# Head of a one-core decoder layer: a third weight tile in a bank of its own and split in pieces, a weight tile moved up in the stream, and products of ones between the first products

## The reference, cut to what matters

```python
def reference(x, c, ..., ada_w, ada_b, norm1_g, w_in, ...):
    sc = jax.nn.silu(c)
    mod = sc @ ada_w[l] + ada_b[l]
    sh1, sc1, g1, sh2, sc2, g2 = [m[:, None, :] for m in jnp.split(mod, 6, axis=-1)]
    xn = rmsnorm(x, norm1_g[l]) * (1.0 + sc1) + sh1          # x is (1, 256, 1024)
    proj = xn @ w_in[l]
    q, k, v, ca, cg = jnp.split(proj, ...)                   # attention: q, k, v; convolution: ca, cg
    ...                                                      # attention over 8 heads
    a = ca * jax.nn.sigmoid(cg)
    a = causal_dwconv(a, conv_dw_w[l], conv_dw_b[l])         # 31 taps
    a = jax.nn.silu(group_norm(a, ...))
    x = x + g1 * (jnp.concatenate([y_attn, a], axis=-1) @ w_out[l])
    xn2 = rmsnorm(x, norm2_g[l]) * (1.0 + sc2) + sh2
    h = causal_dwconv(xn2 @ w_up[l], ...)
    u, g = jnp.split(h, 2, axis=-1)
    return x + g2 * ((jax.nn.silu(g) * u) @ w_down[l])
```

## Time and profile before

| | |
|---|---|
| median of 3 runs | 360.16 us (360.15, 360.16, 363.2) |
| the profiled execution | 365.96 us |
| its span, first to last instruction | 364.2 us |
| mean granted TensorE clock in it | 0.975 of full speed |
| PE busy | 350.2 us, 96% of the span |
| DVE, ACT, POOL busy | 262.5, 177.3, 49.2 us |
| DMA | 79.51 MB, mean 218 GB/s |
| first matmul of conv 2, the end of the head | 46.46 us |

### The profile page before, as it was taken

How to read it: one execution, slowest core, us unless ns; L and a number is a source line. 1 busy time by engine, 2 the same in 40 slices (tenths; PEclk the granted TensorE clock), 3 DMA queues, 4 the chain that set the end, 5 groups by cost and what they waited for, 6 DMA issues and landing times.

```text
span 364.2 us, 6185 instructions
## 1 busy us (share of the span) xinstructions
PE 350.2 (96%) x2425; PEld 299.4 (82%) x2425; DVE 262.5 (72%) x489; ACT 177.3 (49%) x259; POOL 49.2 (14%) x77
## 2 busy tenths in 40 slices
PE   7789999999999998998999999999999999999995
PEld 6557878887664486886998989898989999998984
DVE  2652689979999758648887785766676675858566
ACT  5442662335206484657567645536455463645520
POOL 6362062205001602003200000000000000000000
PEclk9977999999999889999999999999999999999999
DMA  7999947979998991160355556455454554500003
GB/s 281 425 424 422 414 147 297 367 282 342 376 402 289 370 413 53 65 230 2 130 218 200 162 222 226 142 206 193 163 221 142 209 195 165 219 2 1 2 0 115
DMA packets 12797, 79.51 MB, mean 218 GB/s; under 512 B 1368, under 2 KB 2784, under 8 KB 3552
## 3 DMA queue, kind: packets, MB, share of 16 engines
q1 hardware_dynamic: 12560, 78.97, 57.4%
q10 hardware_dynamic: 144, 0.13, 0.1%
q0 software_dynamic: 64, 0.01, 0.0%
HBM read 78.05 MB, written 1.06 MB: 217 GB/s over the span
## 4 chain that ended last, share of the span: by engine, by line
PE 89%; DMA 3%; DVE 3%; issue 2%; ACT 1%; SPq 1%; POOL 0%; DVEq 0%; ACTq 0%; POOLq 0%
PE bank L945 25%; PE bank L946 24%; PE bank L947 24%; PE bank L969 5%; DMA raw<-in_stream 3%; PE bank L1000 2%; PE bank L1202 2%; PE bank L1212 1%; PE bank L1092 1%; DVE w_lo L603 1%; PE bank L1014 1%; PE bank L1238 1%; PE bank L1135 1%; PE bank L1224 1%; PE bank L1145 0%
## 5 line engine op out<-in xcount | busy, mean ns | idle before, releaser
L945 PE MATMUL bank<-act_hi,w_hi 128*128 128x256 f32 x480 | 138.6, 289 | 4.1 <-issue 1.3
L946 PE MATMUL bank<-act_lo,w_hi 128*128 128x256 f32 x480 | 136.6, 285 | 0.0
L947 PE MATMUL bank<-act_hi,w_lo 128*128 128x256 f32 x480 | 136.5, 284 | 0.0
L603 DVE TENSOR_TENSOR w_lo<-raw,w_hi 128x2048 fp32r<-128x2048 f32 (+1 forms) x44 | 95.1, 2161 | 27.6 <-ACT w_hi L374 27.6
L945 PEld LDWEIGHTS bank<-act_hi,w_hi 128*128 128x128 f32 x480 | 92.8, 193 | 12.8 <-issue 9.1
L946 PEld LDWEIGHTS bank<-act_lo,w_hi 128*128 128x128 f32 x480 | 93.0, 194 | 0.4
L947 PEld LDWEIGHTS bank<-act_hi,w_lo 128*128 128x128 f32 x480 | 92.9, 194 | 0.0
L374 ACT ACTIVATE w_hi<-raw 128x2048 fp32r<-128x2048 f32 x45 | 85.8, 1908 | 11.0 <-DMA raw<-in_stream 8.7
L690 DVE SCALAR_TENSOR_TENSOR bank<-glu,cols,bank 128x256 f32<-128x256 f32 x116 | 46.4, 476 | 0.0
L562 ACT ACTIVATE bias<-bank,cols 128x256 f32<-128x256 f32 x44 | 22.2, 556 | 33.9 <-PE bank L947 33.9
L945 PE MATMUL bank<-w_hi,hid_hi 128*128 128x512 f32 x88 | 34.8, 396 | 0.0
(11 more groups left out here) (177 smaller groups left out, 399.2 us busy)
## 6 DMA issues: line engine op xcount, KB each, us to landing
raw<-in_stream SPq DMA_DIRECT2D x71, 1024.0 KB, 6.0
xt<-in_x_t SPq DMA_DIRECT2D x2, 512.0 KB, 4.6
bias<-toeplitz_rows SPq DMA_DIRECT2D x1, 1024.0 KB, 10.7
xr<-in_x_rows SPq DMA_DIRECT2D x1, 1024.0 KB, 8.2
out<-xmod SPq DMA_DIRECT2D x3, 256.0 KB, 2.0
gates_b<-in_ada_b_gates SPq DMA_DIRECT2D x1, 256.0 KB, 8.6
cols<-in_cols SPq DMA_DIRECT2D x1, 185.0 KB, 5.4
out<-xmod SPq DMA_DIRECT2D x1, 128.0 KB, 1.9
```

What stands on the lines that cost most here:

```text
L603: nc.vector.tensor_tensor(w_lo[:, m % PARTS, cut], slot(*SPLIT[m])[:, cut], w_hi[:, m % PARTS, cut].bitcast(f32), ALU.subtract).then_inc(l ...
L945: nc.tensor.matmul(o, sh, mh, start=first, stop=False)
L946: nc.tensor.matmul(o, sh, ml, start=False, stop=False)
L947: return nc.tensor.matmul(o, sl, mh, start=False, stop=last)
```

## The change

- The stream has conv 1 ahead of modulation slot 2, as the fourth slot.
- The squares: ACT squares tiles 4 and 5 as well as 0 to 3, DVE only 6 and 7.
- All `act_lo` of the head go to DVE. POOL has instead the last 768 columns of conv 1 and conv 2 (`POOL_LOW` from 1), and fills the bias rows in one go.
- DVE multiplies `xt` by the inverse norm one part ahead; the low part of conv 0 beyond its first quarter is made after the low parts of `xn` 0 and 1.
- ACT and DVE take conv 1 in pieces at k = 1, and conv 2 in a piece of 768 columns at k = 6 and one of 1280 at k = 7 (ACT), around k = 7 (DVE).
- A sigmoid of a spare element stands on ACT after the last `act_hi`.
- PE has other places for the products of conv 0 and conv 1, with `ada_columns(k)` between them from k = 4 on; part k - 1 follows modulation slot k. `keep_clock` is products of ones, in five places (2, 8, 2, 6 and 2 of them), and the warming ahead of the squares is 10 products.
- conv 2 writes bank 6 and waits for no `glu_ready`.

```diff
-STREAM = [("ada", 0), ("conv", 0), ("ada", 1), ("ada", 2), ("conv", 1),
+STREAM = [("ada", 0), ("conv", 0), ("ada", 1), ("conv", 1), ("ada", 2),
...
-POOL_LOW = range(3, 13)
+POOL_LOW = range(1, 13)
...
+CONV_OF = (0, 1, 6, 1)
+FIRST_PIECE = 3 * SLOT // 8
...
-            for k in range(POOL_LOWS):
-                if 1 <= k <= 3:
-                    fill_rows(buckets[9 * (k - 1):9 * k])
-                pool.wait_ge(xn_full, k + 1)
-                pool.wait_ge(xn_hi, k + 1)
-                nc.gpsimd.tensor_tensor(act_lo[:, k, :], xmod[:, k, :], act_hi[:, k, :].bitcast(f32),
-                                        ALU.subtract).then_inc(xn_lo_pool, 1)
...
+            low_rest(1)
+            fill_rows(buckets)
...
             nc.scalar.activation(xmod[:, 0:KT // 2, :], xt[:, 0:KT // 2, :], ACT.Square).then_inc(xsq_left, 1)
+            act.wait_ge(xt_right, 16)
+            nc.scalar.activation(xmod[:, KT // 2:KT - 2, :], xt[:, KT // 2:KT - 2, :], ACT.Square).then_inc(xsq_right, 1)
...
             copy_rows(0)
-            split_hi_first(0)
-            for k in range(KT):
-                if k == 3:
-                    split_hi_first(1)
-                if k >= 1:
-                    copy_rows(k)
-                if k == KT - 1:
-                    split_hi(FIRST)
+            hi_first_piece(0, PIECE)
+            xn_high(0)
+            hi_other_piece(0, PIECE)
+            copy_rows(1)
+            hi_first_piece(1, PIECE)
+            xn_high(1)
+            hi_other_piece(1, PIECE)
+            for k in range(2, KT):
+                copy_rows(k)
+                if k == KT - 2:
+                    hi_first_piece(FIRST, FIRST_PIECE)
+                elif k == KT - 1:
+                    hi_other_piece(FIRST, FIRST_PIECE)
                 xn_high(k)
+            nc.scalar.activation(spare[:, 0:1], eps[:, :], ACT.Sigmoid)
...
+            xhat(0)
+            xn(0)
+            lo_first_piece(0, PIECE)
+            xn_low(0)
+            xhat(1)
+            xhat(2)
+            xn(1)
+            lo_first_piece(1, PIECE)
+            xn_low(1)
+            lo_other_piece(0, PIECE)
+            xhat(3)
+            lo_other_piece(1, PIECE)
+            xn(2)
+            xn_low(2)
+            for k in range(3, KT):
+                if k + 1 < KT:
+                    xhat(k + 1)
+                xn(k)
+                xn_low(k)
+                if k == KT - 2:
+                    lo_first_piece(FIRST, FIRST_PIECE)
+            lo_other_piece(FIRST, FIRST_PIECE)
...
-                    nc.tensor.transpose(bank[to][:, 0:P], ident[:, :], ident[:, :])
+                    nc.tensor.matmul(bank[to][:, 0:P], ones[:, :], ones[:, :], start=True, stop=True)
...
             ada_rows(0)
+            keep_clock(2, 5)
             ada_columns(0)
-            keep_clock(16, 5)
+            keep_clock(8, 5)
             ada_rows(1)
             first_products(0, (0,))
+            keep_clock(2, 5)
             ada_columns(1)
+            keep_clock(6, 5)
+            first_products(0, (1,))
+            first_products(1, (0,))
             ada_rows(2)
+            first_products(1, (1,))
             ada_columns(2)
-            first_products(1, (0,))
-            first_products(2, (0,))
             ada_rows(3)
-            first_products(0, (1,))
+            keep_clock(2, 2)
             ada_columns(3)
-            first_products(1, (1,))
-            ada_rows(4)
-            first_products(2, (1,))
-            ada_columns(4)
-            for k in range(5, KT):
+            first_products(2)
+            for k in range(4, KT):
                 ada_rows(k)
-                first_products(k - 2)
+                first_products(k - 1, (0,))
                 ada_columns(k)
-            first_products(KT - 2)
+                first_products(k - 1, (1,))
             first_products(KT - 1)
...
-                pe.wait_ge(glu_ready, j - 1)
-                pair(m, j % 2)
+                if j > FIRST:
+                    pe.wait_ge(glu_ready, j - 1)
+                pair(m, CONV_OF[j])
```

More of the change, by code:

```diff
@@ L341, in gn_square @@
                                         conv[:, 2 * g:2 * g + 2, :], ALU.mult).then_inc(gn_sq, 1)
-            for m in POOL_LOW:
+            low_rest(1)
+            fill_rows(buckets)
+            pool.wait_ge(rows_filled, 2 + len(buckets))
+            pool.dma_start(toeplitz_rows, bias_rows[:, :]).then_inc(rows_stored, 16)
+            for m in POOL_LOW[1:]:
                 if m == SP_AT["out", 0]:
@@ L425, in conv_gate @@
                     act.wait_ge(glu_ready, j - 1)
-                nc.scalar.activation(glu_gate[:, j % 2, :], bank[j % 2][:, 0:SEQ], ACT.Sigmoid).then_inc(sig_ready, 1)
+                nc.scalar.activation(glu_gate[:, j % 2, :], bank[CONV_OF[j]][:, 0:SEQ], ACT.Sigmoid).then_inc(sig_ready, 1)
             def qk_raw_out(j):
@@ L656, in norm2_columns, with xhat, xn @@
                 dve.wait_ge(mod_cols_read, 2)
-            for k in range(KT):
+            def xhat(k):
                 nc.vector.tensor_tensor(xt[:, k, :], xt[:, k, :], rinv[:, :], ALU.mult).then_inc(xhat_ready, 1)
+            def xn(k):
                 norm1_columns(k)
@@ L698, in after @@
                     dve.wait_ge(sig_ready, j + 1)
-                    nc.vector.tensor_tensor(glu[:, j, CONV_TAPS - 1:], bank[4 + j if j < FIRST else j % 2][:, SEQ:2 * SEQ],
+                    nc.vector.tensor_tensor(glu[:, j, CONV_TAPS - 1:], bank[4 + j if j < FIRST else CONV_OF[j]][:, SEQ:2 * SEQ],
                                             glu_gate[:, j % 2, :], ALU.mult).then_inc(glu_ready, 1)
@@ L1029, in first_products @@
                     elif k == 2:
-                        ready(m)
+                        pe.wait_ge(lo_done, m + 1)
+                        pe.wait_ge(hi_done, m + 1)
+                    elif k == POOL_FROM // (2 * P) and m in POOL_LOW:
+                        pe.wait_ge(lo_rest, POOL_LOW.index(m) + 1)
                     for c in range(2):
```

47 lines of the change are left out of this document (18 added, 29 removed).

## The result

| | before | changed |
|---|---|---|
| median of 4 runs each | 361.68 us (360.15 to 366.45) | 368.4 us (364.39 to 369.01) |
| the profiled execution | 365.96 us | 368.93 us |
| its span, mean clock | 364.2 us, 0.975 | 366.1 us, 0.977 |
| conv 2's first matmul | 46.46 us | 45.23 us |

A forecast was written before the change was run, and what follows sets the result against it. PE was taken as the bound, with idle gaps and half clock in the head left to win: conv 2 at 42.2 instead of 46.46 us takes 4.3 us off the 360.16 median, giving 356.0 us, range 353.9 to 361.2.

The forecast's parts named there:

- The first product: After slot 1's rows: PE starts at 15.8 us instead of 17.03, a gain of 1.2 us at this point.
- the ones: 20 products in five places of the head: 0.24 us each, 0 us together, or 2 to 3 us at 0.47.
- the clock up to 36 us: Head of PE: granted clock 1.00 from 5 to 36 us, the sum's main step.
- The middle: Conv 1 through part 2: POOL's conv 1 columns beside DVE cost 0.8 us; slot 4 starts between 26.4 and 27.2.
- the second reading of the two: POOL and DVE beside each other on conv 1: each blocks the other, so the middle slips 1.4 us, to 27.8.
- The landing of conv 2: Conv 2 lands at 35.9 us, ACT wants it about 33.7; PE idles up to 1.7 us after slot 7's rows.
- POOL's share of conv 2: POOL's 768 columns start at 38.9 and end between 40.8 and 42.0 us, in time with little to spare.
- The clock behind the gap: Rival, chance 0.13: gaps moved to 36.2 and 39.8 us bring a 3.4 us dip at 0.50, costing 1.7 us: 357.7.
- the slower rival: Chance 0.09: clock falls behind ACT's wait for conv 2, which starts at 47.1 to 48.2; 360.8 to 361.9 us, or 365.5.
- Carrying the 4.3 us over to the median: Head gain taken off the 360.16 us median, 5.8 us below the profiled execution: 355.9, say 356.0 us.
- The first rival: Chance 0.24: median runs of before lack the head's dip, so the change gives -0.4 to +1.1 us, 359 to 360.6.
- The sum over the profiled execution: Conv 2 starts at 42.2 instead of 46.46, 4.3 us off the head: 365.96 - 4.3 = 361.7 us.

The follow-up runs named there:

- e8: The changed kernel without POOL's shares of conv 1 and conv 2, whose low parts DVE makes alone; median 363.83 us.
- e1: The changed kernel with conv 2's last 768 low-part columns made by DVE, not POOL; median 365.29 us, ratio to before 1.0075.
- e7: e2 plus conv 2 in pieces, in banks 6 and 3, started at its first piece, and the sigmoid of a spare element; median 363.82 us.
- e6: The kernel before, run again with no edit; median 365.90 us.
- e12: e7 with every `act_lo` of the head on DVE and POOL filling the bias rows in one go; median 364.10 us, ratio to before 1.0023.
- e2: The kernel before with products of ones as PE's fillers, 8 replacing 16 transposes and more in three head gaps; median 363.81 us, ratio 1.0058.
- e3: The changed kernel with two transposes in place of each `keep_clock` product of ones; median 367.38 us, ratio to before 1.0173.
- e5: The changed kernel, run again with no edit; median 367.38 us.
- e9: The changed kernel with nine more products of ones in the gap ahead of part 7; median 364.42 us, ratio to before 1.0060.
- e11: e7 with conv 1 ahead of modulation slot 2 in the stream; median 364.80 us, ratio to before 1.0047.
- e4: The kernel before with eight products of ones (about 2.0 us) ahead of conv 2; median 364.48 us, ratio 1.0080.
- e10: e7 with the squares of tiles 4 and 5 moved to ACT; median 364.36 us, ratio to before 1.0047.

## Why the prediction was wrong

**The first product, the ones, the clock up to 36 us: right.** 15.8 forecast, 15.72 measured. Sixteen instructions of ones take 2.03 us, 0.25 a product, at the low end of the 0.24 to 0.47. The granted clock reads 1.00 from 5 us up to the fall at 42.7.

**The middle: right in kind and near in size.** POOL's 768 columns of conv 1 start at 20.10, while DVE's 1536 columns run (19.25 to 21.0), and take 2.58 us, against 1.81 for the same work at 39.42; DVE's step on `xt`, started at 20.92, takes 2.04 in place of 0.42 and ends 0.3 us behind POOL's:

```profile
20.10 2.58 POOL L324 TENSOR_TENSOR w_lo<-raw,w_hi 128x768 fp32r<-128x768 f32 x1 [12.52 <-ACT w_hi L408]
```

```profile
20.92 2.04 DVE L671 TENSOR_TENSOR xt<-xt,rinv 128x256 f32<-128x256 f32 x1
```

So each waited for the other in turn, the second reading of the two. But the share also spares DVE 768 columns (0.95 us for 1.75), and its price on the chain is 0.7 us, the start of part 2's products here against e8, close to my 0.8 and not 1.4. Slot 4 starts at 27.36, between my 27.2 and the 27.8 by that rule. The rounds take 3.1 us each in place of 2.97, and slot 7 comes at 36.66, just past 35.2 to 36.6.

**The landing of conv 2: right.** It comes at 36.11 (forecast 35.9), and PE's gap behind slot 7's rows is 0.39 us, inside "up to 1.7". ACT waits 1.05 us for it and not 2.2, as it asks at 35.06 instead of 33.7.

**POOL's share of conv 2: the step that failed first.** I asked only whether its 768 columns "are in time, with little to spare". They were. I didn't ask what they hold up, though the same text had the collision of conv 1 in it. DVE's scale step at 39.6 and what needs it, `act_hi` 7 on ACT and the low part on DVE, are the path to part 7. The scale took 1.55 us for 0.16, and part 7 came at 42.62 instead of 40.7: 1.4 us of these 1.9 are the collision (e1). Of the rest, 0.3 us is that columns 7 start at 38.91 and not 38.6, behind a landing 0.2 us later, and 0.2 that the steps from there to part 7 take 2.3 us even in e1, against 2.1 in the sum. What the middle lost was covered by the wait ahead of part 6. I had named "if POOL's share of conv 1 or conv 2 holds PE" as a sign of being wrong, but gave it no price and no rival. The Trainium skill, SBUF — State Buffer, section "SBUF: two separate sides", says that a GpSimd operation that reads SBUF and a DVE operation with two inputs in SBUF lock each other out for a whole instruction, whichever starts first. The trace agrees: both of DVE's stretched steps have two such inputs and end with POOL's or within 0.3 us behind it, and the step with one input in PSUM, right beside the long one, took 0.15 (L648). It shows also that the size of DVE's step doesn't matter: one column waits as long as 256.

**The clock behind the gap: a rival, met at another price.** I gave 0.13 to a fall of 3.4 us behind the moved gaps. It came, at 42.7 to 46.1, behind 2.39 us rather than 1.7 or 0.9, and stretched the twelve products of part 7 from 1.51 (39.97 to 41.48 in e7) to 2.61 us. Together with the collision it puts conv 2 at 45.23, 3.0 us behind the forecast of 42.2. The mechanism of the slower rival, a fall behind ACT's wait for the landing, wasn't met: the wait was 1.05 us, below the 2 us from which I let it decide. My own sum had 2.2 us for it (33.7 to 35.9), so by my own words this rival should have decided, and I gave it 0.09.

**Carrying the 4.3 us over to the median: the second step that failed.** The first rival (0.24) said that the runs at 360.16 have no dip in the head, and that conv 2 would then start at 41.8. e6 shows such an execution, with conv 2 at 42.18. The clocks say so for the runs near 360.16 too: all eleven of before between 359.9 and 360.7 us whose clock is on record have a mean of 0.994, which leaves room for one stretch of 3.4 us at 0.50 (e7 has that mean, and its one stretch in attention), while the fall of the head in before's profile lasts 10.2 us. From there even a perfect change, at 42.2, wins nothing, and the changed kernel without any fall would be at 42.62 + 1.51 = 44.1, nearly 2 us later than before. Without the collision it is at 42.5 (e1), still no earlier than before. The runs say the same: at a mean clock of 0.990 the span is 360.1 us before and 362.0 changed (one run), at 0.977 364.1 and 365.4. The rival was right in its premise and not in its price, -0.4 to +1.1 us of gain, as it left out the collision too. I argued against it with "the gaps are in the program, not in the profiler". But neither the fall nor the first gap, the 1.26 us, is in every execution (e6).

**The sum over the profiled execution.** Forecast 361.7, measured 368.93, so 7.2 us off. Conv 2 gives 3.0, the end of the fall behind it 0.3, attention 2.8, and the time outside the span 1.1 (2.83 in place of 1.76). For the median, 368.4 against 356.0, the 5.8 us that were carried over come on top, less 0.5 by which the profiled run is longer than the median. The chances don't add up as the text says either: by its own rule "same" gets 0.495 and not 0.48, "slower" 0.045 and not 0.06.

**What stays open.** I took what lies behind the head to be the same in both kernels. In every profile but e12's the clock falls between 113 and 149 us, and it isn't the same: its time at 0.50 there is 3.4 us in e7, 6.8 in before, e1 and e2, 10.2 in e6, 13.6 to 13.7 in the changed kernel, e3, e5, e8, e9 and e11, and 17.1 in e4 and e10. Before and e6 are one program and differ by 3.4. The long sum comes with the changed kernel's gap (e3, e5) and without it (e8, e9, e11), so nothing ties it to that gap. What sets it wasn't found, and no run moves this stage alone; the 2.8 us lost there in the profiled execution may be the draw of that execution. What decides whether the head of before falls, beyond that the two executions with the fall have the first gap and e6 hasn't, is open as well.

## What to carry to other kernels

When work is given to POOL, ask not only whether it is done in time but which DVE instruction stands next while it runs: a step of one column on the critical path can cost the whole of POOL's instruction. Where POOL and DVE meet within a tenth or two of a us, look at several traces: which starts first can change from run to run. A fall of the clock that one execution has and another of the same program hasn't is no gain to be sold: price a change from the executions without it, and compare runs at equal mean clock. Where a change mixes a means (ones) with a new order, run the means alone: on the old order it gave conv 2 at 42.19, with none of the new collisions.
